# Input loads in order of need, rotated key channels on a second queue, and a last chunk that two engines normalise and one queue stores in four parts

## The chip, the cores and the metric

The kernel runs on one core of one Trainium2 chip. The metric is the device time of one execution in microseconds (us), lower is better. TensorE is called PE in the rows, VectorE DVE, ScalarE ACT, GpSimd POOL; SP is SyncE, which here only issues transfers. A row's L538 is line 538 of the kernel's source, and `out<-in` names the tensors.

## What is computed

One inference step of a two-layer decoder trunk in float32, for a prompt of 1024 tokens and 8 samples of 4 new tokens each, 1056 token columns in all. Cut to what matters:

```python
for l in range(2):                       # x <- LayerNorm(alpha * x + sublayer(x))
    z = x @ w_in                         # 1024 -> 22 (layer 0) or 37 (layer 1) tiles of 128 columns
    # layer 0: latent attention, linear recurrence, memory attention
    # layer 1: mLSTM, chunk MLP, memory attention
    x = layer_norm(alpha * x + mixed @ w_out, ln_g[l], ln_b[l])

# layer 0, the samples' latent attention over 16 pages of 128 cached tokens each:
def page_step(carry, pt):                # lat 256 channels, kr 32 rotated channels
    lat, kr = lat_pool[e, pt], rope_pool[e, pt]
    s = q_lat @ lat.T + q_rope @ kr.T
    return _softmax_accumulate(carry, s, lat), None
```

## The kernel before

Activations lie with channels on the 128 partitions (8 tiles `k`) and tokens along the columns, in three chunks `c` of 352 tokens. A float32 product is made of three matmuls: every operand is split into a rounded `hi` part (ACT) and the rest `lo` (DVE), and PE adds hi·hi, lo·hi and hi·lo (L538 to L540, L592 to L594). Each engine's program is written out by hand in its order; semaphores tie them together.

**Start.** PE's first products need `x_hi` and `x_lo` of chunk 0 and the first weight tile. SP loads chunk 0 of `x_raw` whole and then weights. POOL loads chunks 1 and 2, then six constants and the recurrence's weights `lru_w`. ACT and DVE split a chunk at a time. `pe_slot(t, c)` makes output tile `t` of chunk `c`; the order is (0, 0), (0, 1), (0, 2), (1, 0) and so on.

**Samples' latent attention** (`pe_mla_sample`). Ten events `EV`: in each group of four samples one for the new tokens and four for cached pages, each of those with 4 pages of 4 samples, numbered `r` = 0 to 7. For event `r` SP issues 16 page loads into one of three buffers (`pages[r % 3]`), once the values product of event `r - 3` is done (`ss_o`). A page row holds 256 latent and 32 rotated channels. PE first turns the pages over (`turn`, units `w` of 512 columns, moved out of PSUM by ACT and DVE in turn): 8 units of latent and a ninth, `w == 8`, of 16 small matmuls for the rotated channels (`ropeT`). Iteration `e` of the loop on PE is `turn(e+1)`, `transposes(e)`, `scores(e+1)`, `values(e)`.

**LayerNorm** of a chunk: PE sums the channels by a matmul with ones (`"sum"`, L731), DVE centres two halves of four tiles (L760), ACT squares them (L789), the squares are summed, ACT takes the root (L792), DVE the reciprocal (L769), DVE scales the halves (L772), ACT applies gain and bias tile by tile (L797). For chunks 0 and 1 DVE adds the 8 squared tiles first (L765, L766) and PE needs one matmul (L737); for the last chunk of each layer PE sums all 8 tiles itself (L742). In layer 0 the products (30, 0) stand between `"sum"` and `"square"` of that chunk, and (30, 1), (31, 0), (31, 1) behind them; (30, 2) waits for the whole normalised chunk 2. In layer 1 nothing is left beside this chain, and POOL stores each chunk of `y` whole, the last one as the program's last transfer.

Of the kernel before, what the change touches and what calls it, by code (L numbers as in the profile page):

```python
# [28 lines left out]
P = 128  # L29
# [112 lines left out]
def build(nc, x, o):  # L142

    with ExitStack() as ctx:
# [91 lines left out]
        page01 = keep("page", [P, 2, 4, 4, 288])  # L236
        latT = keep("latT", [P, 4, 2, 512])
        ropeT = keep("ropeT", [P, 512])
# [7 lines left out]
        page2 = place("page2", [P, 4, 4, 288], Z0 + 10 * ROWS)  # L246
# [112 lines left out]
        x_in = [sem(f"x_in{c}") for c in range(NCH)]  # L359
# [19 lines left out]
        lru_in = sem("lru_in")  # L379
# [30 lines left out]
        smp_in = sem("smp_in")  # L410
# [116 lines left out]
        def pe_slot(pe, t, c):  # L527
# [3 lines left out]
            if t in (0, 30, 31):  # L531
                pe.wait_ge(x_ready, NCH if t else c + 1)
                if t:
                    pe.wait_ge(x_ready, NCH + 2 * c + 2)
# [76 lines left out]
        def act_x_hi(act, c):  # L611

            act.activation(x_hi[:, :, chunk(c)], x_raw[:, :, chunk(c)], ACT.Copy).then_inc(x_hi_ready, 1)

        def dve_x_lo(dve, c):
            dve.wait_ge(x_hi_ready, c + 1)
            dve.tensor_tensor(x_lo[:, :, chunk(c)], x_raw[:, :, chunk(c)], x_hi[:, :, chunk(c)],
                              ALU.subtract).then_inc(x_ready, 1)
# [96 lines left out]

        def norm_at(table, n):

            return [(c, piece) for c in range(NCH - 1) for piece in table.get(n - KX * (c + 1), ())]
# [6 lines left out]
        def pe_norm(pe, l, c, what):  # L725
# [6 lines left out]
            else:  # L732
                if n:
                    pe.wait_ge(ln_r, n)
                if c < NCH - 1:
                    pe.wait_ge(ln_t, 2 * l + c + 1)
                    pe.matmul(bank(7, n=CH), ones[:, :], ln_sum[:, c % 2, :], start=True, stop=True).then_inc(ln_v, 1)  # L737
                    return
# [13 lines left out]
        def dve_norm_pieces(dve, v, l):  # L752
            def piece(c, what):
# [7 lines left out]
                elif what.startswith("sum"):  # L761
                    if c < NCH - 1:
# [3 lines left out]
                        dve.tensor_tensor(ln_sum[:, c % 2, :], ln_sq[:, 0, :], ln_sq[:, 1, :], ALU.add).then_inc(ln_t, 1)  # L766
                elif what == "root":
                    dve.wait_ge(ln_r, n + 1)
                    v.then(dve.reciprocal(root, root))  # L769
                elif what.startswith("scale"):  # L770
                    dve.wait_ge(ln_c, 2 * n + 2)
                    dve.tensor_tensor(r, r, wide(root), ALU.mult).then_inc(ln_n, 1)  # L772
                elif l == 0:
                    dve.wait_ge(x_hi_ready, NCH + 2 * c + h + 1)
# [4 lines left out]
        def act_norm_pieces(act, l):  # L779
            out = x_next if l == 0 else res  # L780

            def piece(c, what):
# [11 lines left out]
                elif what.startswith("affine"):  # L794
                    act.wait_ge(ln_n, 2 * n + h + 1)
                    for m in range(4 * h, 4 * h + 4):
# [401 lines left out]
        def pe_lru(pe, i, w):  # L1198
            j = LRU_ORDER[i]
            pe.wait_ge(lru_in, 16)  # L1200
# [71 lines left out]
        def dve_conv_edges(dve, v):  # L1272
            dve.wait_ge(z_free, ZI[(3, 2)])
            dve.wait_ge(branch_in, 32)
# [311 lines left out]
        def unit_out(n):  # L1586
            r, w = n // 9, n % 9
            if w == 8:
                return ropeT[:, :]
            return latT[:, w // 2, :, 256 * (w % 2):256 * (w % 2) + 256]  # L1590

        def unit_in(n):
            b = bank(UNIT_BANKS[n % 3])
            return b if n % 9 == 8 else b.rearrange("p (k c) -> p k c", k=2)

        def pe_mla_sample(pe):
# [3 lines left out]
            def turn(e):  # L1600
# [3 lines left out]
                for w in range(9):  # L1604
                    n = 9 * r + w
# [5 lines left out]
                    if w == 8:  # L1611
# [1351 lines left out]
```

## Time and profile before

| | us |
|---|---|
| median of three runs | 1580.4 (1580.4 to 1581.9) |
| the profiled execution, its own time | 1582.64 |
| its span, first to last event | 1580.9 |
| PE busy in the span | 1476.9 (93%) |
| DVE, ACT, POOL busy | 784.7, 577.5, 38.2 |

The span is what the rows count from. The other 1.74 us of the profiled execution lie outside it. Busy time of PE is modelled and pipelined, so 93% doesn't say that all of it is needed.

### The profile page before, as it was taken

How to read it: one execution, taken by the hardware profiler on the slowest of the kernel's cores; microseconds unless marked ns; L12 is line 12 of the kernel's file. 1: busy time of each engine (PE TensorE's matmuls, PEld its weight loads, DVE VectorE, ACT ScalarE, POOL GpSimd, SP SyncE). 2: the span in 40 equal slices, each digit the busy share in tenths (PEclk: the TensorE clock that was granted, in tenths of full speed). 3: DMA queues.
4: the chain of work that ended last, by engine and by line, in shares of the span. 5: the costliest groups of instructions: out<-in, count | busy, mean ns of one | idle time of the engine just before them, and what ended most of it. 6: DMA issues, size and time to landing. Idle time of an engine off the chain costs nothing.

```text
span 1580.9 us, 24315 instructions
## 1 busy us (share of the span) xinstructions
PE 1476.9 (93%) x10022; PEld 1298.7 (82%) x10022; DVE 784.7 (50%) x1444; ACT 577.5 (37%) x1030; POOL 38.2 (2%) x68
## 2 busy tenths in 40 slices
PE   5999999999999888889998999999999999999993
PEld 5988999866666565559997798999999989989992
DVE  3475643164554554555784143324444358526674
ACT  3057312144545554342453123204444115212343
POOL 1000000000000000000000100000000001000000
PEclk9999999999999999999998999999999899999997
DMA  5110032220001061735554230120011121114552
GB/s 198 42 40 28 28 108 94 74 82 13 1 1 54 1 185 49 203 124 167 168 191 165 94 107 28 49 52 27 28 30 57 70 81 41 42 39 149 170 190 73
DMA packets 51920, 132.13 MB, mean 84 GB/s; under 512 B 6601, under 2 KB 30394, under 8 KB 51042
## 3 DMA queue, kind: packets, MB, share of 16 engines
q1 hardware_dynamic: 46114, 111.45, 22.6%
q0 software_dynamic: 5696, 19.12, 3.3%
q8 instruction: 80, 1.31, 0.3%
q14 instruction: 30, 0.25, 0.1%
HBM read 117.08 MB, written 13.47 MB: 83 GB/s over the span
## 4 chain that ended last, share of the span: by engine, by line
PE 53%; DVE 3%; issue 2%; ACT 2%; POOL 0%; DVEq 0%; POOLq 0%; ACTq 0%
PE ps L538 9%; PE ps L540 9%; PE ps L539 9%; PE ps L592 4%; PE ps L593 4%; PE ps L594 4%; PE ps L1620 2%; PE ps L2051 1%; PE ps L1129 1%; PE ps L1645 1%; DVE ln_sq L769 1%; PE ps L2243 1%; PE ps L1917 1%; PE ps L1373 1%; PE ps L1915 1%
## 5 line engine op out<-in xcount | busy, mean ns | idle before, releaser
L538 PE MATMUL ps<-x_hi,w_hi 128*128 128x352 f32 x1416 | 472.8, 334 | 22.5 <-DVE w_lo L488 20.0
L540 PE MATMUL ps<-x_hi,w_lo 128*128 128x352 f32 x1416 | 458.6, 324 | 0.0
L539 PE MATMUL ps<-x_lo,w_hi 128*128 128x352 f32 x1416 | 458.1, 324 | 0.0
L538 PEld LDWEIGHTS ps<-x_hi,w_hi 128*128 128x128 f32 x1416 | 269.2, 190 | 32.0 <-DVE w_lo L488 20.3
L539 PEld LDWEIGHTS ps<-x_lo,w_hi 128*128 128x128 f32 x1416 | 270.0, 191 | 2.5 <-issue 1.2
L540 PEld LDWEIGHTS ps<-x_hi,w_lo 128*128 128x128 f32 x1416 | 268.8, 190 | 0.0
L482 ACT ACTIVATE w_hi<-w_raw 128x1024 fp32r<-128x1024 f32 (+1 forms) x107 | 123.3, 1152 | 311.0 <-PE ps L540 201.9
L488 DVE TENSOR_TENSOR w_lo<-w_raw,w_hi 128x1024 fp32r<-128x1024 f32 (+1 forms) x107 | 143.5, 1341 | 64.6 <-ACT w_hi L482 64.0
L592 PE MATMUL ps<-mx_hi,w_hi 128*128 128x352 f32 x480 | 158.1, 329 | 1.5 <-DVE mx_lo L679 1.2
L594 PE MATMUL ps<-mx_hi,w_lo 128*128 128x352 f32 x480 | 154.4, 322 | 0.0
L593 PE MATMUL ps<-mx_lo,w_hi 128*128 128x352 f32 x480 | 154.4, 322 | 0.0
L514 DVE COPY z<-ps 128x352 f32<-128x352 f32 x90 | 47.1, 524 | 194.2 <-PE ps L540 194.2
L502 ACT ACTIVATE sig<-ps 128x352 f32<-128x352 f32 x72 | 33.4, 464 | 200.4 <-PE ps L540 200.4
L592 PEld LDWEIGHTS ps<-mx_hi,w_hi 128*128 128x128 f32 x480 | 90.5, 189 | 3.0 <-DVE mx_lo L679 1.3
L593 PEld LDWEIGHTS ps<-mx_lo,w_hi 128*128 128x128 f32 x480 | 90.9, 189 | 0.8
L594 PEld LDWEIGHTS ps<-mx_hi,w_lo 128*128 128x128 f32 x480 | 90.4, 188 | 0.0
L516 DVE TENSOR_TENSOR mx<-sig,ps 128x352 f32<-128x352 f32 x54 | 28.1, 520 | 122.8 <-ACT sig L502 122.6
L918 ACT ACTIVATE probs<-ps,stat 128x1024 f32<-128x1024 f32 (+7 forms) x64 | 47.4, 741 | 98.2 <-DVE stat L948 97.7
L869 PE MATMUL ps<-kT,qT 96*128 96x512 f32 (+4 forms) x192 | 75.5, 503 | 0.5 <-ACT qs L2656 0.5
L881 PEld LDWEIGHTS ps<-ident,probs 128*128 128x128 f32 x288 | 32.8, 141 | 35.8 <-ACT probs L918 25.9
L881 PE MATMUL ps<-ident,probs 128*128 128x128 f32 x288 | 43.2, 277 | 16.5 <-ACT probsT L929 8.5
L601 DVE SCALAR_TENSOR_TENSOR res<-x_res,ps 128x352 f32<-128x352 f32 x48 | 24.9, 519 | 54.0 <-PE ps L594 54.0
(456 smaller groups left out, 1887.7 us busy)
## 6 DMA issues: line engine op xcount, KB each, us to landing
w_raw<-in_w_out SPq DMA_DIRECT2D x48, 640.0 KB, 3.9
w_raw<-in_w_in SPq DMA_DIRECT2D x59, 512.0 KB, 3.6
page<-in_cache_mla SPq DMA_DIRECT2D x128, 144.0 KB, 2.6
kvs<-in_mem_cache SPq DMA_DIRECT2D x16, 512.0 KB, 6.0
x_res<-in_xT SPq DMA_DIRECT2D x24, 176.0 KB, 2.4
x<-x_next POOLq DMA_DIRECT2D x3, 1408.0 KB, 8.1
x_res<-x SPq DMA_DIRECT2D x24, 176.0 KB, 2.3
out_y<-res POOLq DMA_DIRECT2D x3, 1408.0 KB, 5.9
```

The costliest lines, as they stand in the source:

```text
L482: act.activation(w_hi[:, u % 2, 0:n], w_raw[:, u % 2, 0:n], ACT.Copy).then_inc(w_hi_ready, 1)
L488: dve.tensor_tensor(w_lo[:, u % 2, 0:n], w_raw[:, u % 2, 0:n], w_hi[:, u % 2, 0:n], ALU.subtract).then_inc(w_split, 1)
L514: ins = dve.tensor_copy(out, zz[0:8] if tile.one else zz)
L538: pe.matmul(out, w_hi[:, u % 2, kk], x_hi[:, k, chunk(c)], start=(k == 0), stop=False)
L539: pe.matmul(out, w_hi[:, u % 2, kk], x_lo[:, k, chunk(c)], start=False, stop=False)
L540: mm = pe.matmul(out, w_lo[:, u % 2, kk], x_hi[:, k, chunk(c)], start=False, stop=(k == KX - 1))
L592: pe.matmul(out, w_hi[:, u % 2, kk], mx_hi[:, k, chunk(c)], start=(k == 0), stop=False)
L593: pe.matmul(out, w_hi[:, u % 2, kk], mx_lo[:, k, chunk(c)], start=False, stop=False)
L594: mm = pe.matmul(out, w_lo[:, u % 2, kk], mx_hi[:, k, chunk(c)], start=False, stop=(k == KM - 1))
L869: mm = pe.matmul(s[:, a:b], q_of(u), k_of(u, a, b), start=True, stop=True)
L881: mm = pe.transpose(ps[:, 4 + f % 2, (kt - k0) * P:(kt - k0 + 1) * P], pr[:, kt * P:(kt + 1) * P], ident[:, :])
L918: act.activation(probs_of(n, u), scores_of(n, u), ACT.Exp, bias=stat[:, n % 4:n % 4 + 1], scale=MLA_SCALE, accum_out=stat[:, 4 + n % 4:5 + ...
```

## The change

1. **Start.** The input comes in four parts (`X_PARTS`): tiles 0 to 3 of chunk 0, tiles 4 to 7 of chunk 0, chunk 1, chunk 2. All are issued by SP, with the first weight tile behind the first part and the second behind chunk 1. ACT and DVE split part by part; PE starts (0, 0) on part 0 and waits for part 1 before tile `k == 4`. POOL begins with the constants; `lru_w` and two small loads wait until the last input part has landed.
2. **Rotated channels.** The page rows are 256 wide. The rotated channels lie in an array of their own, laid out channels first, so they need no turning. POOL loads them, 128 transfers of 32 rows by 512 bytes, into three buffers, each group of four behind a read of page numbers into registers. The ninth unit is gone from PE, ACT and DVE.
3. **Squares.** For the last chunk DVE adds the squares, each half as soon as ACT has it (five instructions), and PE does one matmul.
4. **Last chunk of layer 1** (`LAST`). DVE scales tiles 0 to 3 as before and tile 4; tiles 5 to 7 it scales and biases itself. ACT does tiles 0 to 4. SP stores the last chunk of `y` in four parts, in the order in which they are ready.

```diff
+        X_PARTS = [(0, slice(0, 4)), (0, slice(4, KX)), (1, slice(0, KX)), (2, slice(0, KX))]
@@ pe_slot
+                if (t, c, k) == (0, 0, 4):
+                    pe.wait_ge(x_ready, 2)
@@ pe_norm, "square"
-                for m in range(KX):
-                    if m % 4 == 0:
-                        pe.wait_ge(ln_q, 2 * n + m // 4 + 1)
-                    mm = pe.matmul(bank(7, n=CH), ones[:, :], ln_sq[:, m, :], start=(m == 0), stop=(m == KX - 1))
-                mm.then_inc(ln_v, 1)
+                pe.wait_ge(ln_t, n + 1)
+                pe.matmul(bank(7, n=CH), ones[:, :], ln_sum[:, c % 2, :], start=True, stop=True).then_inc(ln_v, 1)
@@ dve_norm_pieces
+                    else:
+                        for g in range(2):
+                            dve.wait_ge(ln_q, 2 * n + g + 1)
+                            for a in (2, 1):
+                                v.then(dve.tensor_tensor(ln_sq[:, 4 * g:4 * g + a, :], ln_sq[:, 4 * g:4 * g + a, :],
+                                                         ln_sq[:, 4 * g + a:4 * g + 2 * a, :], ALU.add))
+                        dve.tensor_tensor(ln_sum[:, c % 2, :], ln_sq[:, 0, :], ln_sq[:, 4, :], ALU.add).then_inc(ln_t, 1)
+                elif what == "scale1" and (l, c) == LAST:
+                    dve.tensor_tensor(res[:, 4, chunk(c)], res[:, 4, chunk(c)], root, ALU.mult).then_inc(ln_n, 1)
+                    for m in range(A_TILES, KX):
+                        v.mark(dve.scalar_tensor_tensor(res[:, m, chunk(c)], res[:, m, chunk(c)],
+                                                        vec[:, V_LNG + KX * l + m:V_LNG + KX * l + m + 1], root,
+                                                        ALU.mult, ALU.mult))
+                    v.settle()
+                    for m in range(A_TILES, KX):
+                        dve.tensor_scalar(res[:, m, chunk(c)], res[:, m, chunk(c)],
+                                          vec[:, V_LNB + KX * l + m:V_LNB + KX * l + m + 1], None,
+                                          ALU.add).then_inc(ln_t, 1)
@@ pe_mla_sample, turn
-                    if w == 8:
-                        for q in range(4):
-                            for j in range(4):
-                                mm = pe.matmul(ps[32 * j:32 * j + 32, b, q * P:q * P + P],
-                                               pages[r % 3][:, q, j, LAT:LAT + ROPE], ident[:, :],
-                                               start=True, stop=True)
@@ pe_mla_sample, scores
+                pe.wait_ge(rp_in[real(e) % 3], 256 * (real(e) // 3 + 1))
@@ sync
+            for a, b, ready, n in ((0, 2, ln_y, KX * (2 * NCH - 1) + 2), (5, 7, ln_t, 2 * NCH + 2),
+                                   (2, 5, ln_y, KX * (2 * NCH - 1) + 5), (7, 8, ln_t, 2 * NCH + 3)):
+                sp.wait_ge(ready, n)
+                sp.dma_start(o["y"][:, a:b, chunk(NCH - 1)], res[:, a:b, chunk(NCH - 1)]).then_inc(out_done, 16)
+            sp.wait_ge(out_done, 64)
@@ gpsimd
-            for c in range(1, NCH):
-                gp.dma_start(x_raw[:, :, chunk(c)], x["xT"][:, :, chunk(c)]).then_inc(x_in[c], 16)
...
+            gp.wait_ge(x_in[3], 16)
+            gp.dma_start(lru_w, x["lru_w"].rearrange("p j w n -> p j (w n)")).then_inc(branch_in, 16)
...
+            gp.wait_ge(o_ready, len(PAIRS))
+            for r in range(8):
+                if r >= 3:
+                    gp.wait_ge(ss_o, 5 * ((r - 3) // 4) + 2 + (r - 3) % 4)
+                for j in range(4):
+                    n = (4 * (r // 4) + j) * NPG + 4 * (r % 4)
+                    _, four = nc.values_load_multi_w_load_instructions(
+                        table[0:1, n:n + 4], engines=[mybir.EngineType.Pool], min_val=0, max_val=NPHYS - 1,
+                        skip_runtime_bounds_check_because="a page table holds numbers of pages")
+                    for q in range(4):
+                        gp.dma_start(ropeT[32 * j:32 * j + 32, r % 3, q * P:q * P + P],
+                                     x["cache_rope"][bass.ds(four[q], 1), :, :].rearrange(
+                                         "a c p -> (a c) p")).then_inc(rp_in[r % 3], 16)
```

SP's program begins like this before the change (`w_raw` is a weight tile, two buffers):

```order
L2471 DMA x_raw<-in_xT 128x8x352
L474 DMA w_raw<-in_w_in 128x1024 [waits w_split] x16
L2477 DMA memT0a<-in_memT 128x1024 [waits lat_ready,conv_ready]
L2477 DMA memT0b<-in_memT 128x1024
L474 DMA w_raw<-in_w_in 128x1024 [waits w_split] x6
```

and like this after it:

```order
L2481 DMA x_raw<-in_xT 128x4x352
L474 DMA w_raw<-in_w_in 128x1024 [waits w_split]
L2481 DMA x_raw<-in_xT 128x4x352
L2484 DMA x_raw<-in_xT 128x8x352
L474 DMA w_raw<-in_w_in 128x1024 [waits w_split]
L2486 DMA x_raw<-in_xT 128x8x352
```

The whole input is now on SP's queue, in the order in which PE uses it. On PE, the iteration of the samples' attention with the second page event reads before the change:

```order
L1645 MATMUL ps<-latT,qs 32x512 x8
L1649 MATMUL ps<-ropeT,qsr 32x512 x4
L1675 MATMUL ps<-lat_tm,sp_selfT 32x256 x4
L1620 MATMUL ps<-ident,page 128x128 x32
L1614 MATMUL ps<-ident,page 32x128 x16
L1662 MATMUL ps<-ident,sp_p 128x128 x4
```

and after it, with L1654, L1658, L1684, L1628 and L1671 as the new numbers of L1645, L1649, L1675, L1620 and L1662:

```order
L1654 MATMUL ps<-latT,qs 32x512 x8
L1658 MATMUL ps<-ropeT,qsr 32x512 x4
L1684 MATMUL ps<-lat_tm,sp_selfT 32x256 x4
L1628 MATMUL ps<-ident,page 128x128 x32
L1671 MATMUL ps<-ident,sp_p 128x128 x4
```

Only the row of 16 small matmuls is gone. POOL's program after the change, from the stores of the prompt's memory keys and values to the first of the 128 loads of rotated channels:

```order
L1171 DMA out_mem_k<-km_90 128x2x256 [waits mem_ev]
L1172 DMA out_mem_v<-vm 128x2x256
L2593 DMA out_kr<-z 32x1056 [waits kr_ready]
L2601 TENSOR_LOAD table [waits o_ready,tbl_in]
L2605 ISA
L2605 DMA ropeT<-in_cache_rope 32x128
```

The last two rows stand four times behind each TENSOR_LOAD, and there are 32 such groups, four for each page event; the ISA row works out the address in registers. Before the change the store of `kr` was followed on POOL by the stores of `x_next`.

## Rows read from the trace of the kernel before

**Rows 1.** The page, part 4: shares of the chain that ended last, by engine.
```profile
PE 53%; DVE 3%; issue 2%; ACT 2%; POOL 0%; DVEq 0%; POOLq 0%; ACTq 0%
```

**Rows 2.** Timeline of the start: start us, us, engine, line, operation, [idle before <-releaser].
```profile
1.39 1.94 POOL L2553 DMA_DIRECT2D x_raw<-in_xT  x2 [0.86 <-POOLq L2937]
...
11.30 2.55 ACT L613 ACTIVATE x_hi<-x_raw 128x2816 fp32r<-128x2816 f32 x1 [9.21 <-DMA x_raw<-in_xT]
...
16.97 1.22 DVE L488 TENSOR_TENSOR w_lo<-w_raw,w_hi 128x1024 fp32r<-128x1024 f32 x1
18.10 6.19 DVE L617 TENSOR_TENSOR x_lo<-x_raw,x_hi 128x2816 fp32r<-128x2816 f32 x2
...
18.24 0.66 PE L538 MATMUL ps<-x_hi,w_hi 128*128 128x352 f32 x1 [18.24 <-DVE w_lo L488]
...
32.81 0.53 DVE L514 COPY z<-ps 128x352 f32<-128x352 f32 x1 [3.32 <-PE ps L540]
```

**Rows 3.** A window of 1 us: busy times, granted PE clock, DMA share, GB/s.
```profile
10.00:11.00 1.00, 0.00 (x0) 0.00 (x0) 0.00 (x0) 0.00 (x0) 0.00 (x0) 1.00 0.99 367
```

**Rows 4.** Timeline of one iteration of the samples' attention.
```profile
629.14 1.08 PE L1614 MATMUL ps<-ident,page 128*32 128x128 f32 x32
629.25 0.69 DVE L1779 COPY latT<-ps 128x512 f32<-128x512 f32 x1 [0.22 <-PE ps L1620]
...
630.15 0.66 PE L1662 MATMUL ps<-ident,sp_p 128*128 128x128 f32 x4
...
630.99 1.92 PE L1645 MATMUL ps<-latT,qs 128*32 128x512 f32 x16 [0.18 <-issue]
```

**Rows 5.** Page loads of `r = 3` and `r = 7`, last turn and scores; reads of numbers.
```profile
625.46 14.47 SPq L2515 DMA_DIRECT2D page<-in_cache_mla  x24
...
677.19 0.86 SPq L2515 DMA_DIRECT2D page<-in_cache_mla  x2
...
689.65 1.86 PEld L1620 LDWEIGHTS ps<-ident,page 128*128 128x128 f32 x16 [0.26 <-DMA page<-in_cache_mla]
...
693.67 1.92 PE L1645 MATMUL ps<-latT,qs 128*32 128x512 f32 x16 [0.32 <-DVE ropeT L1779]
...
L2504 SPq TENSOR_LOAD <-table x32: 293/296/504, 558.1 to 666.0; - x32
```

**Rows 6.** POOL's small transfers: timeline, then KB each and us to landing.
```profile
868.12 0.51 POOL L2584 DMA_DIRECT2D g_i<-gates  x1 [1.88 <-DMA gates<-mx]
...
g_i<-gates POOLq DMA_DIRECT2D x4, 4.0 KB, 1.8
g_f<-gates POOLq DMA_DIRECT2D x4, 4.0 KB, 5.1
```

**Rows 7.** Timeline of layer 0's normalisation: chunk 1's adds, then chunk 2.
```profile
809.11 2.54 DVE L765 TENSOR_TENSOR ln_sq<-ln_sq 128x1408 f32<-128x1408 f32 x2
...
834.10 3.15 DVE L760 SCALAR_TENSOR_TENSOR res<-ps,res 128x1408 f32<-128x1408 f32 x2
...
837.27 7.99 PE L742 MATMUL ps<-ln_sq,ones 128*128 128x352 f32 x16 [2.68 <-ACT ln_sq L789]
...
859.24 0.40 PE L538 MATMUL ps<-x_hi,w_hi 128*128 128x352 f32 x1 [2.53 <-DVE x_lo L775]
```

**Rows 8.** Timeline of the end, all engines.
```profile
1549.80 3.15 DVE L760 SCALAR_TENSOR_TENSOR res<-ps,res 128x1408 f32<-128x1408 f32 x2 [0.95 <-PE ps L731]
...
1552.98 6.66 PE L742 MATMUL ps<-ln_sq,ones 128*128 128x352 f32 x16 [3.22 <-ACT ln_sq L789]
...
1562.65 3.16 DVE L772 TENSOR_TENSOR res<-res,ln_sq 128x1408 f32<-128x1408 f32 x2
1564.31 4.68 ACT L797 ACTIVATE res<-res,vec 128x352 f32<-128x352 f32 x8 [4.08 <-DVE res L772]
1569.29 0.84 POOL L2550 DMA_DIRECT2D out_y<-res  x1 [17.91 <-ACT res L797]
```

**Rows 9.** DMA issues from 1545 us on: count, KB each, median us to landing.
```profile
out_y<-res POOLq DMA_DIRECT2D x2, 1408.0 KB, 5.9
```

More of the change, by code:

```diff
@@ L235, in build @@
         cursor[0] = X0
-        page01 = keep("page", [P, 2, 4, 4, 288])
+        page01 = keep("page", [P, 2, 4, 4, LAT])
+        ropeT = keep("ropeT", [P, 3, 512])
         latT = keep("latT", [P, 4, 2, 512])
-        ropeT = keep("ropeT", [P, 512])
         sp_p = keep("sp_p", [P, 2, 512])
@@ L409, in build @@
         pgT_ev = [sem("pgT_ev_a"), sem("pgT_ev_v")]
-        smp_in = sem("smp_in")
+        rp_in = [sem(f"rp_in{c}") for c in range(3)]
         l96_in = sem("l96_in")
@@ L609, in dve_step, with x_part, act_x_hi, dve_x_lo @@
                 dve.tensor_tensor(total, first, res[:, t, chunk(c)], ALU.add).then_inc(ln_a, 1)
[L611 to L618, printed above, removed]
+        def x_part(buf, n):
+            c, k = X_PARTS[n]
+            return buf[:, k, chunk(c)]
+        def act_x_hi(act, n):
+            act.wait_ge(x_in[n], 16)
+            act.activation(x_part(x_hi, n), x_part(x_raw, n), ACT.Copy).then_inc(x_hi_ready, 1)
+        def dve_x_lo(dve, n):
+            dve.wait_ge(x_hi_ready, n + 1)
+            dve.tensor_tensor(x_part(x_lo, n), x_part(x_raw, n), x_part(x_hi, n), ALU.subtract).then_inc(x_ready, 1)
         MX_ORDER = [4, 5, 6, 7, 8, 9, 0, 1, 2, 3]
@@ L795, in piece @@
                     act.wait_ge(ln_n, 2 * n + h + 1)
-                    for m in range(4 * h, 4 * h + 4):
+                    for m in range(4 * h, A_TILES if h and (l, c) == LAST else 4 * h + 4):
                         act.activation(out[:, m, chunk(c)], res[:, m, chunk(c)], ACT.Identity,
@@ L1603, in turn @@
                 r = real(e)
-                for w in range(9):
-                    n = 9 * r + w
+                for w in range(8):
+                    n = 8 * r + w
                     if w in (0, 4):
@@ L1648, in scores @@
                     rr = slice(32 * j, 32 * j + 32)
-                    mm = pe.matmul(ps[rr, e % 2, :], rows_of(qsr[rr], g, j), ropeT[rr, :], start=False, stop=True,
+                    mm = pe.matmul(ps[rr, e % 2, :], rows_of(qsr[rr], g, j), ropeT[rr, real(e) % 3, :], start=False, stop=True,
                                    skip_group_check=True)
@@ L1725, in units @@
                     return
-                first = 9 * real(e)
-                for n in range(first + first % 2, first + 9, 2):
+                first = 8 * real(e)
+                for n in range(first, first + 8, 2):
                     act.wait_ge(pgT_z, n + 1)
@@ L1775, in units @@
                     return
-                first = 9 * real(e)
-                for n in range(first + 1 - first % 2, first + 9, 2):
+                first = 8 * real(e)
+                for n in range(first + 1, first + 8, 2):
                     dve.wait_ge(pgT_z, n + 1)
@@ L2614, in _ @@
             gp.dma_start(o["chunk_v"], vd_s[:, :]).then_inc(cv_out, 16)
-            for c in range(NCH):
+            for c in range(NCH - 1):
                 gp.wait_ge(ln_y, KX * (NCH + c + 1))
@@ L2684, in _ @@
             v.then(dve.memset(eps[:, :], EPS))
-            for c in range(NCH):
-                dve_x_lo(dve, c)
-                if c == 0:
+            for n in range(len(X_PARTS)):
+                dve_x_lo(dve, n)
+                if n == 0:
                     dve_lo(dve, 0)
```

70 lines of the change are left out of this document (34 added, 36 removed).

## Prediction

> **What bounds the kernel now.** I read the chain of waits first: PE's own work is more than half of it and no other engine has more than 3% [rows 1], and the idle time left on PE lies in a few places. So time can be won only where PE waits or does work that another can take, and at both ends, where PE does nothing yet or any more. The timelines of four such places matter; reading down each of them, one looks for the row whose idle time names the releaser.
>
> *Start.* ACT can split chunk 0 only at 11.30, when the whole chunk has landed. Then x_hi, x_lo and w_lo follow one another, and PE begins at 18.24 [rows 2]. Meanwhile POOL's two 1.44 MB loads share the transfer engines with SP's. The transfers run at 367 GB/s together [rows 3]. Before 11.30 about 3.1 MB have to pass, chunk 0, as much of POOL's, and the constants' first part, so data begin near 3 us. The copy of the third slot starts at 32.81 [rows 2], so tile 1 begins about then; from there on PE has work.
>
> *Samples' attention.* PE does the turning, the transposes, the scores and the values one after another with next to no gap. The 16 small matmuls of the ninth unit run from 629.14 until the transposes begin at 630.15 [rows 4].
>
> *Layer 0's last chunk.* PE needs 7.99 us for the sum of squares, and three tiles and 15 us later it waits 2.53 us for `x_lo` of that chunk [rows 7].
>
> *End.* Centre to 1552.95, PE's squares, root, reciprocal, scale, affine, one POOL store at 1569.29 that lands 5.9 us later, at about 1575.2 [rows 8, 9]. The span ends 5.7 us after that, and I take this tail as fixed.
>
> **The change, part by part.**
>
> *Start.* Bytes in SP's order: part 0 0.72 MB, w0 0.52, part 1 0.72, chunk 1 1.44, w1 0.52, chunk 2 1.44; POOL's constants (0.27 MB) share the first of them. From 3.0 us at about 380 GB/s they land at about 6.0, 7.4, 9.2, 13.0, 14.4 and 18.2. A whole chunk costs ACT 2.55 and DVE 3.09, w_lo costs DVE 1.22 [rows 2]; half a chunk I take at half. So x_hi is ready at 7.4, x_lo at 9.0, w_hi at 8.5, w_lo at 10.2, and PE starts at about 10.3 instead of 18.24. That is not the gain, since it runs into later parts. Chunk 1: landed 13.0, x_hi 15.6, x_lo 18.7. Chunk 2: landed 18.2, x_hi 20.7, x_lo 23.8. Slot (0, 2) can begin at 23.9 and takes 24 x 0.16 = 3.9 us, ends at 27.8, where before it was about 32.8: **4.9 us**. w1 waits behind chunk 2 on ACT and DVE (x_lo ends 23.8, w_lo by 25.2), before 27.8. If a transfer is a microsecond late the gain is 3.9. Moving `lru_w` behind the input costs nothing: the recurrence needs it tens of microseconds later.
>
> *Ninth unit.* 630.15 - 629.14 = 1.01 us of PE goes in each of 8 turns. The scores behind it then wait for the last latent unit: DVE's copy ends at 629.94 [rows 4], the transposes, started 1.01 earlier, end at 629.8. So the scores begin at 629.99 instead of 630.99, and nearly all of it is kept: 8 x 1.01 = 8.1 us. What is late next is the page load. A load may start when the values of `r - 3` are done; for the last event SP issues its 16 loads from 677.19 on, two in 0.86 us, and PE already waits 0.26 us for the second half at 689.65 [rows 5]. Between the two PE now saves one more unit (1.01), while the loads, bound by SP's issue and not by their bytes, are hardly quicker. That wait grows by 1.0. The event `r = 3` has some 1 us to spare by the same count. Net: **7.1 us** (8.1 if the smaller pages are quicker).
>
> *Rotated channels on POOL.* This operation is not in the trace. A small POOL transfer takes 0.51 us, landing 1.8 to 5.1 us [rows 6]. A read of four page numbers takes SP 0.29 to 0.50 us [rows 5]. Per event there are 16 issues and 4 reads; C is what they take together. Lower bound, if all register work hides behind the issues: 16 x 0.51 = 8.2 us. Upper bound from these rows: SP's page loads take 0.33 each and start 0.53 apart (the second of two ends 0.86 after the first begins [rows 5]), so 0.2 lies between them; 16 x 0.71 + 4 x 0.5 = 13.4. I take the middle for the issue and the short read, 16 x 0.61 + 4 x 0.3 = 11, since both are the same kind of work on the same kind of sequencer, and landing L = 3. POOL may begin an event when SP may. For r = 7 that was 677.19 and the scores came at 693.67 [rows 5], 16.5 us later; two units go from between, 14.4 are left, the same for r = 3. Needed: 11 - 0.5 + 3 = 13.5, just in time. The backlog: from r = 3's start at 625.46 to the last scores there were 68.2 us, six units fewer make 62.1, and POOL's last transfer lands 5C - 0.5 + L after that start if events queue up. PE is then late by 5C + L - 62.6: nothing for C = 11, from C = 11.9 on 5 us for each microsecond. I take **0 us**; 7 at C = 13.4, and 9 with a landing of 5.1. What waits behind it on POOL, the stores of `x_next`, comes 90 us later.
>
> The Trainium skill, "DMA: Bandwidth & Descriptors", section "Latency and other measured facts", gives a register read from memory a floor of about 600 ns. By it C would be 12.2 and PE 1.4 us late, an estimate from that page; the rows say 0.29 to 0.50, so the sum doesn't take it.
>
> *Squares.* Two adds of 1408 and 704 columns take 2.54 us [rows 7], one of 1408 takes 1.6 [rows 8], so 704 costs 0.92; 352 columns cost 0.53 [rows 2]. 2 x (0.92 + 0.53) + 0.53 = 3.45 after the centre, then one matmul of about 0.9. Layer 0: the centre ends at 837.25, so the sum is there at 841.6 instead of 845.26: 3.6 us earlier. PE's own three tiles then start at 841.3 and take 11.6 us, perhaps 1.5 more if the granted clock is the lower one after the idle time, so they end by 854.4, before `x_lo` at 855.6: **3.6 us**. Bounds 2 to 5, the upper if PE's shorter wait before (30, 2) spares it a stretch at the lower clock. Layer 1: 1552.95 + 3.45 + 0.9 = 1557.35 instead of 1559.64: **2.3 us**.
>
> *Scaling and store.* From the reciprocal on, before: two halves, 3.16, and 8 affines beside them, the last done at 1568.99 [rows 8], 6.3 us after the scaling began. Now ACT has 5 (1.6 + 5 x 0.585 = 4.6) and DVE 1.6 + 0.53 + 3 x 0.53 + 3 x (0.26 to 0.53) = 4.5 to 5.3. Gain 1.3. The store: POOL's whole one took 5.9 us from an issue 0.3 behind. Now a first part is on its way 2 us before, and 1.08 MB of the 1.44 follow within a microsecond: at 370 GB/s 2.9 us and a start of 1.2, about 4.2 from the last issue. Gain 1.7. **3.0 us** (1 to 4).
>
> Sum: 4.9 + 7.1 + 0 + 3.6 + 2.3 + 3.0 = 20.9. From the profiled execution's 1582.6 that is 1561.7; the median of the runs shown lies 2.2 below that execution, so 1580.4 - 20.9 = **1559.5**.
>
> **Rivals.**
>
> *Forecast:* POOL keeps up. For it: small issues of 0.5 us, and the first three events have 40 us. 0.57.
>
> *POOL falls behind a little.* C = 12.5 to 15.5: 5C + 3 - 62.6 = 3 to 18 us come back, time 1562 to 1577, at C = 14 1570. The upper end is beyond the bound above, since no row shows register work on POOL. For it: POOL's address work has no row, and three page events and one with new tokens run behind one another. 0.23. The Trainium skill, "SBUF — State Buffer", section "SBUF: two separate sides", says that descriptors of POOL's transfers are not written while DVE runs a copy from SBUF to SBUF in its two-port mode. DVE's copies in this stage read PSUM, so by it nothing changes here; it could fall on the first groups only.
>
> *Slower.* Each issue with its register work takes 0.95 us, as POOL's big ones do (two in 1.94 [rows 2]): C = 15.2 + 4 x 0.4 = 16.8, late by 24, minus 20.9 gives 1584. It decides from C = 16.2 on. Against it: those moved 1024 rows each, these 32. 0.05.
>
> *Less at the ends.* The transfers at the start are issued by one queue and cannot keep 380 GB/s, the parts land 2 us later, and four stores take as long as one: 4 to 5 us less, 1564. 0.08.
>
> *More.* No low clock behind the shorter waits, smaller pages load quicker: 1556. 0.07.
>
> **The numbers.** Two runs differ by up to 0.1%; 0.2% (3.2 us, 1577.2 to 1583.6) is what tells a change from none. Faster: 0.57 + 0.07 + 0.08 + nearly all of 0.23, and 0.93 in all; within 0.2%: 0.02; slower: 0.05. The range takes in the forecast (1557 to 1562), the better case and POOL's lateness up to C = 14: 1555 to 1570.
>
> **What would show it.** PE's first matmul near 10.3 and the third slot's copy near 27.8; no ninth unit and no wait of PE on `ropeT`; a wait on `page` of about 1.3 us at the last turn; POOL's issues 0.5 to 0.65 us apart, with C readable from one event; layer 0's single L737-like matmul ending near 841.6 less what went before; in the end 4.2 us from SP's last issue to landing. The prediction is wrong if POOL's pitch passes 0.7 us, if loads on two queues slow the pages, or if the 5.7 us behind the last landing depend on which queue stored.

## The result and the profile after

| | before | after |
|---|---|---|
| median, us | 1580.94 (4 runs, 1580.4 to 1581.9) | 1563.91 (4 runs, 1561.34 to 1566.23) |
| ratio | | 0.9893, 95% interval 0.9879 to 0.9907 |
| profiled execution, span | 1580.9 | 1564.6 |
| PE busy | 1476.9 | 1462.9 |
| POOL busy | 38.2 | 99.2 |

The change is worth 17.0 us in the median and 16.3 in the two spans. The forecast was 1559.5, 4.4 below the result, with 20.9 us as its sum. That looks close, but the terms are not: in these two traces the samples' attention gave 1.5 us for a term of 7.1, and the end gave twice its terms, through something that the prediction had called fixed.

The timeline of the start of the changed kernel, as in [rows 2], and the copy of the third slot behind it:

```profile
5.63 1.38 ACT L619 ACTIVATE x_hi<-x_raw 128x1408 fp32r<-128x1408 f32 x1 [3.42 <-DMA x_raw<-in_xT]
...
8.66 1.22 DVE L488 TENSOR_TENSOR w_lo<-w_raw,w_hi 128x1024 fp32r<-128x1024 f32 x1
...
9.93 0.66 PE L540 MATMUL ps<-x_hi,w_hi 128*128 128x352 f32 x1 [9.93 <-DVE w_lo L488]
...
18.93 2.56 ACT L619 ACTIVATE x_hi<-x_raw 128x2816 fp32r<-128x2816 f32 x1 [2.63 <-DMA x_raw<-in_xT]
...
29.05 0.52 DVE L514 COPY z<-ps 128x352 f32<-128x352 f32 x1 [2.17 <-PE ps L542]
```

PE starts at 9.93 instead of 18.24, and the third slot's copy stands at 29.05 instead of 32.81. That is a lead of 3.8 us, and only this lead counts.

The last turns of the samples' attention, PE's timeline, against the last two of [rows 5]:

```profile
664.40 1.92 PE L1654 MATMUL ps<-latT,qs 128*32 128x512 f32 x16 [0.55 <-DVE latT L1788]
...
674.13 1.92 PE L1654 MATMUL ps<-latT,qs 128*32 128x512 f32 x16 [0.55 <-DVE latT L1788]
...
681.76 2.00 PE L1628 MATMUL ps<-ident,page 128*128 128x128 f32 x16 [0.91 <-DMA page<-in_cache_mla]
...
687.14 3.35 PE L1654 MATMUL ps<-latT,qs 128*32 128x512 f32 x16 [2.94 <-DMA ropeT<-in_cache_rope]
```

And GpSimd's issues, which feed that last row:

```profile
661.93 1.07 POOL L2605 DMA_DIRECT2D ropeT<-in_cache_rope  x2 [0.43 <-issue]
663.34 1.08 POOL L2605 DMA_DIRECT2D ropeT<-in_cache_rope  x2 [0.34 <-issue]
670.20 2.22 POOL L2605 DMA_DIRECT2D ropeT<-in_cache_rope  x4 [5.77 <-PE ps L1686]
...
680.67 0.50 POOL L2605 DMA_DIRECT2D ropeT<-in_cache_rope  x1 [0.19 <-issue]
```

Three things are to be seen. A turn now takes 9.7 us (664.40 to 674.13) where it took 10.5. The scores of `r = 7` stand 2.94 us for their rotated channels, and the 16 matmuls behind that wait take 3.35 us in place of 1.92: the granted clock is 0.55 from 687.0 to 690.4, close to the lower of TensorE's two levels. And GpSimd was not slow. It stood idle for 5.77 us before it could begin `r = 7`, released by L1686, the weighted sum of `r = 4` (reading the first page numbers is part of this time). The 16 issues of the event take it 11.0 us (670.20 to 681.17), and PE goes on 6.5 us after the last of them began.

The end, all engines, against [rows 8]:

```profile
1544.16 3.16 DVE L760 SCALAR_TENSOR_TENSOR res<-ps,res 128x1408 f32<-128x1408 f32 x2 [0.95 <-PE ps L738]
...
1547.23 1.44 DVE L771 TENSOR_TENSOR ln_sq<-ln_sq 128x704 f32<-128x704 f32 x2
...
1550.32 0.52 DVE L773 TENSOR_TENSOR ln_sum<-ln_sq 128x352 f32<-128x352 f32 x1
1550.99 1.51 PE L743 MATMUL ps<-ln_sum,ones 128*128 128x352 f32 x2 [6.86 <-DVE ln_sum L773]
1552.54 0.55 ACT L810 ACTIVATE ln_sq<-ps,eps 128x352 f32<-128x352 f32 x1 [3.81 <-PE ps L743]
...
1557.17 2.97 ACT L815 ACTIVATE res<-res,vec 128x352 f32<-128x352 f32 x5 [4.08 <-DVE res L790]
...
1558.45 2.86 SPq L2561 DMA_DIRECT2D out_y<-res  x4
1559.09 1.03 DVE L785 TENSOR_SCALAR res<-res,vec 128x352 f32<-128x352 f32 x3
```

And what the transfer engines moved in the last 7 us, 1558 to 1565, in 40 slices of 0.175 us:

```profile
GB/s 0 0 0 0 0 0 0 56 346 378 362 370 370 177 0 80 362 330 330 394 354 370 370 378 362 378 386 386 378 362 346 330 266 16 0 0 0 0 0 0
```

The last byte passes at about 1563.8 (in the 34th slice), and the span ends at 1564.6. In the kernel before, the same view of 1571 to 1581 has its last byte at 1574.8, and the span ends at 1580.9. So of the 10.7 us that the end gained (27.95 us from the centring's end to the span's end before, 17.3 after), 5.3 are what lay behind the last byte, 6.1 before and 0.8 after.

### The profile page after: what moved, and what is told of

Its sections match the earlier page's. It is cut to its first block, busy times and chain, and to the rows that moved or that the text cites. A ratio compares the mean times of both kernels' runs of the same rounds, so it can differ in the third digit from the quotient of the medians.

```text
span 1564.6 us, 24181 instructions
## 1 busy us (share of the span) xinstructions
PE 1462.9 (93%) x9738; PEld 1290.3 (82%) x9738; DVE 789.8 (50%) x1457; ACT 573.9 (37%) x1024; POOL 99.2 (6%) x193
## 4 chain that ended last, share of the span: by engine, by line
PE 82%; DVE 8%; ACT 4%; issue 4%; DMA 1%; SPq 1%; POOLq 0%; POOL 0%; ACTq 0%; DVEq 0%
PE ps L540 14%; PE ps L542 14%; PE ps L541 14%; PE ps L594 4%; PE ps L596 4%; PE ps L595 4%; PE ps L887 2%; PE ps L911 2%; PE ps L1147 2%; PE ps L899 2%; DVE stat L965 1%; PE ps L1628 1%; PE ps L2821 1%; PE ps L2060 1%; PE ps L2830 1%
## 5 line engine op out<-in xcount | busy, mean ns | idle before, releaser
L2605 POOL DMA_DIRECT2D ropeT<-in_cache_rope x128 | 63.6, 497 | 285.8 <-issue 239.1
```

The source lines that it names most:

```text
L2605: gp.dma_start(ropeT[32 * j:32 * j + 32, r % 3, q * P:q * P + P], x["cache_rope"][bass.ds(four[q], 1), :, :].rearrange("a c p -> (a c) p") ...
```

## Experiments

Every kernel ran beside the kernel before on the same chip. On one chip single times of the kernel before lie up to 9.6 us apart (1576.38 to 1585.99), so small differences are read from the traces as well, at the same place in the program; a trace is one execution, and where it and the median disagree, the text says so.

### Whose tail is it?

Four kernels ask what the 6 us behind the last byte belong to.

`y_on_sp`, the kernel before with one store moved:

```
             sp_steps(sp, 1)
+            sp.wait_ge(ln_y, 2 * KX * NCH)
+            sp.dma_start(o["y"][:, :, chunk(NCH - 1)], res[:, :, chunk(NCH - 1)]).then_inc(out_done, 16)
+            sp.wait_ge(out_done, 16)
...
-            for c in range(NCH):
+            for c in range(NCH - 1):
                 gp.wait_ge(ln_y, KX * (NCH + c + 1))
                 store(o["y"][:, :, chunk(c)], res[:, :, chunk(c)])
```

> The kernel before, with one edit: the last chunk of y is still scaled as before and stored whole, but by SyncE. Theory A (5.7 us tail of a GpSimd store, 0.3 of one of SyncE): 5 to 6 us faster than before, 1575 us. Rival C (the tail belongs to any end of the program): within 1 us of before, 1580 us.

`pool_waits`, the changed kernel with one wait more:

```
             gp.wait_ge(gout_done, n_out[0])
+            gp.wait_ge(out_done, 64)
```

> The changed kernel, whose GpSimd waits at its very end for the four stores of y that SyncE issued, as SyncE does. Between the last byte of y and the end of the span lay some 5.7 us in the kernel before (last store issued by GpSimd) and some 0.3 us in the changed one. Theory A (the 5.7 us belong to a store that GpSimd's queue carries): no change against the changed kernel, end of the span within 0.6 us of the last landing. Rival B (GpSimd is slow to finish once its last wait is met, whoever issued the store): 4 to 6 us slower than the changed kernel, 1568 to 1570 us.

`four_on_pool`, the changed kernel, the four stores and their waits moved from SyncE's program to the end of GpSimd's stores, where they count on `gout_done`:

```
...
-                sp.wait_ge(ready, n)
-                sp.dma_start(o["y"][:, a:b, chunk(NCH - 1)], res[:, a:b, chunk(NCH - 1)]).then_inc(out_done, 16)
-            sp.wait_ge(out_done, 64)
...
+                gp.wait_ge(ready, n)
+                n_out[0] += 16; gp.dma_start(o["y"][:, a:b, chunk(NCH - 1)], res[:, a:b, chunk(NCH - 1)]).then_inc(gout_done, 16)
```

> The changed kernel, whose four parts of the last y are issued by GpSimd, with the same waits in the same order. GpSimd's issue of a large store lasts 0.85 us, SyncE's some 0.4 to 0.9. Theory A (a store of GpSimd's queue has some 5 us behind its last byte): 5 to 8 us slower than the changed kernel, 1569 to 1572 us, with 5 to 6 us between the last landing and the span's end. Rival C (the end is shorter because it is cut in parts and two engines scale, as the prediction had it, with the queue worth nothing): within 2 us of the changed kernel.

`sp_waits`, the kernel before, the last store still GpSimd's, but counted on `out_done`, for which SyncE waits and GpSimd doesn't:

```
+            sp.wait_ge(out_done, 16)
...
-            for c in range(NCH):
+            for c in range(NCH - 1):
...
+            gp.wait_ge(ln_y, 2 * KX * NCH)
+            gp.dma_start(o["y"][:, :, chunk(NCH - 1)], res[:, :, chunk(NCH - 1)]).then_inc(out_done, 16)
```

> The kernel before: GpSimd stores the last y whole as before, but SyncE waits for its landing in place of GpSimd, whose own last wait is for the earlier stores. So far: GpSimd stores and waits, 6.2 us from the last byte to the span's end; SyncE stores and waits, 0.8 us; SyncE stores, both wait, 7.2 us. Theory A (GpSimd needs 6 to 7 us to finish after its last instruction, and overlaps them with the store here): GpSimd is through with its issue at 1570.1 and finishes at 1576 to 1577, SyncE at 1576: 4 to 5 us faster than before, 1575 to 1577 us. Rival B (what is late is a GpSimd queue that has just carried a store): no change, 1580 us.

| kernel | stores | waits for it | last byte | span's end | between | median, ratio to before |
|---|---|---|---|---|---|---|
| before | GpSimd | GpSimd | 1574.8 | 1580.9 | 6.1 | |
| y_on_sp | SyncE | SyncE | 1573.3 | 1574.1 | 0.8 | 1574.47, 0.9959 (0.9945 to 0.9972) |
| after | SyncE | SyncE | 1563.8 | 1564.6 | 0.8 | 1563.91, 0.9893 |
| pool_waits | SyncE | both | 1562.3 | 1569.5 | 7.2 | 1570.70, 0.9935 (0.9918 to 0.9952) |
| four_on_pool | GpSimd | GpSimd | 1561.8 | 1569.3 | 7.5 | 1572.24, 0.9948 (0.9928 to 0.9967) |
| sp_waits | GpSimd | SyncE | 1574.4 | 1577.8 | 3.4 | 1579.04, 0.9995 (0.9982 to 1.0008) |

`pool_waits` decides between the two theories of the first three, and against the one that I had put first. Nothing about the stores differs from the changed kernel there; only GpSimd waits for them too. The end of that kernel, 1560 to 1570, in slices of 0.25 us:

```profile
GB/s 383 372 372 366 372 366 377 355 344 113 0 0 0 0 0 0 0 0 0 0 0 0 0 0 0 0 0 0 0 0 0 0 0 0 0 0 0 0 0 0
```

The transfers are over in the tenth slice, and the span goes on for 7.2 us in which no engine has a row. So the time belongs to GpSimd's own finish after its last wait, and not to a store on its queue. What GpSimd does in it no row shows. `sp_waits` is the converse and half a confirmation. GpSimd's last row is its issue, which ends at 1569.89, and the span ends 7.9 us later; had the tail begun at the last byte (1574.4), the end would be at 1580.5. From the start of that issue to the end of the span it took 8.7 us there and 11.6 before, 2.9 less, where 4 to 5 were expected. The median moved by 0.6 us alone, within an interval that reaches from 2.8 us faster to 1.3 slower, so the 2.9 us rest on the two traces. A GpSimd that issues the last store still ends late. Moving the store and the wait together is what paid: 5.3 us behind the last byte in `y_on_sp`, and about 6 in its median, as theory A had it.

### Each part by itself

The kernel before with one part of the change's diff at a time, word for word. Only in the last one two counts differ, since `ln_t` has two increments fewer without the third part:

```
-            for a, b, ready, n in ((0, 2, ln_y, KX * (2 * NCH - 1) + 2), (5, 7, ln_t, 2 * NCH + 2),
-                                   (2, 5, ln_y, KX * (2 * NCH - 1) + 5), (7, 8, ln_t, 2 * NCH + 3)):
+            for a, b, ready, n in ((0, 2, ln_y, KX * (2 * NCH - 1) + 2), (5, 7, ln_t, 2 * NCH),
+                                   (2, 5, ln_y, KX * (2 * NCH - 1) + 5), (7, 8, ln_t, 2 * NCH + 1)):
```

> The kernel before with the first part of the change alone: input in four parts in order of need, constants and lru_w from GpSimd. The prediction had 4.9 us for it (3.9 if a transfer is late); the changed kernel's trace shows its third slot's copy at 29.05 in place of 32.81, 3.8 us, and the same lead still there at 600. Theory A (that lead is kept to the end): 3.5 to 4 us in the trace at every mark, 1576 to 1577 us. Rival B (the lead is lost where a transfer is the limit): less than 2 us at the end of the span.

> The kernel before with the second part alone: pages without rotated channels, these loaded by GpSimd. From the first turning matmul to the first matmul of the out-projection the stage took 106.1 us before, 104.6 in the changed kernel and 99.8 where the buffer is freed by the scores. Theory A (the late release of the buffer eats the gain): 103 to 106 us for the stage, a wait of 2 to 4 us on ropeT at the last turn, and 1 to 3 us faster in all. Rival B (only together with the other parts is it late, since they move when loads meet): 99 to 101 us for the stage, 5 to 7 us faster in all.

> The kernel before with the third part alone: VectorE adds the last chunks' squares, TensorE sums one tile. The prediction had 3.6 us in layer 0 and 2.3 in layer 1, 5.9 in all. In the changed kernel layer 0 gained 2.9 us up to the root, 4.4 up to the gates' store and again 2.9 from 900 on. Theory A: 2.9 us kept from layer 0 and 2.3 to 3 from layer 1, 1574 to 1576 us. Rival B (what PE saves it waits for later): under 1.5 us from layer 0, 1577 to 1579 us.

> The kernel before with the fourth part alone: the last third scaled by two engines and stored in four parts by SyncE. From the end of the centring to the span's end it took 27.9 us before and 17.3 in the changed kernel, of which adding the squares on VectorE is some 2.7. Theory A (GpSimd needs some 6 us to finish after its last wait, SyncE under 1): 19.5 to 20.5 us, 8 us faster, 1572 to 1573 us. The prediction's sum (tail fixed, 1.3 + 1.7 us): 3 us faster, 1577 us.

| kernel | median | ratio to before | us |
|---|---|---|---|
| start_only | 1578.72 | 0.9993 (0.9981 to 1.0004) | -1.7 |
| rope_only | 1580.31 | 0.9992 (0.9977 to 1.0008) | -0.1 |
| squares_only | 1577.71 | 0.9987 (0.9976 to 0.9998) | -2.7 |
| end_only | 1571.63 | 0.9940 (0.9918 to 0.9962) | -8.8 |

The fourth part has more than half of the gain, and the rotated channels on GpSimd give nothing that the medians can show (from 3.6 us faster to 1.3 slower), where 1 to 3 us were expected. The four add up to 13.3 us, the whole gives 17.0; each has 1.7 to 3.5 us of uncertainty, so this is no contradiction, nor a proof that they are independent.

In `start_only` the lead is 4.4 us at the first store of the conv state (65.12 against 69.53), 5.8 at 201, 3.9 at 904 and 2.2 at the end. It grows and shrinks in stretches of code that are the same in both. The windows between two of GpSimd's stores, before and `start_only` (us; PE, PEld, DVE, ACT, POOL busy; PEclk, DMA share, GB/s):

```profile
1220.42:1294.91 74.49, 74.49 (x417) 67.31 (x416) 36.21 (x58) 8.60 (x13) 1.31 (x3) 0.91 0.18 61
```

```profile
1216.52:1292.69 76.17, 76.17 (x417) 68.97 (x416) 36.22 (x58) 8.60 (x13) 1.31 (x2) 0.89 0.17 60
```

The same 417 matmuls, PE without a pause in both, take 1.7 us longer at a mean granted clock of 0.89 than at 0.91. So in the trace rival B (a transfer is the limit) is not what took the lead. Over the 14 profiles of this study, all with this same code, the stretch took 74.5 to 74.6 us in seven and 76.0 to 76.2 us in seven.

The median says less than theory A expected: 1.7 us, and its interval ends at 3.0. The runs' clocks say where some of the lead may have gone. The ten runs of `start_only` have mean granted clocks of 0.975 to 0.979, 0.9767 on average, the 25 of before on the same chip 0.977 to 0.984, on average 0.9799; and among those 25 a clock lower by 0.001 goes with a time 1.0 us longer. By these numbers the lower clock costs `start_only` some 3 us (an estimate). `squares_only` has 0.9767 too, `rope_only` 0.9792. Why a kernel whose start is earlier meets the lower clock more often is not shown.

`rope_only` confirms that the wait comes with the second part alone: 2.5 us on `ropeT` at the last turn, 1.3 on `page`, the stage 102.0 us.

`squares_only` has layer 0's 2.85 us as the changed kernel (between GpSimd's second and third store of `x_next` 22.06 us against 24.90, and 22.05 after). In layer 1 the time from the second to the third store of `y` went from 18.76 to 17.19: 1.6 us. That is 4.4 us in the trace, where the median has 2.7 (interval 0.3 to 3.8), a value that rival B had named. The other traces show why the first number is not a fixed one. With the squares added on VectorE the stretch in layer 0 takes 22.05 to 22.10 us in every trace. With the 16 matmuls it takes 24.9 us in four traces and 23.6 and 23.4 in `end_only` and `rope_only`, where the 16 matmuls ran in 6.7 and 6.5 us in place of 8.0 (mean granted clock 0.75 in `end_only`, 0.62 in before). So this part is worth 2.85 us or 1.4 in layer 0, as the clock falls. `end_only` took 19.6 us from centring to the span's end, inside the 19.5 to 20.5 of theory A, and 3 us faster is excluded.

### The wait on the rotated channels

`rope_free` is the changed kernel with one word changed. The last reader of a `ropeT` buffer is the scores (`ss_z`); the weighted sum (`ss_o`) comes 10 us later and reads the page only:

```
                 if r >= 3:
-                    gp.wait_ge(ss_o, 5 * ((r - 3) // 4) + 2 + (r - 3) % 4)
+                    gp.wait_ge(ss_z, 5 * ((r - 3) // 4) + 2 + (r - 3) % 4)
```

> The changed kernel; GpSimd's rotated channels of page group r wait for the scores of group r-3 (the last reader of the ropeT buffer) and no longer for its weighted sum. In the changed kernel's trace the group r=7 was issued only from 670.20, after 5.77 us of waiting for the weighted sum of r=4, took 11.0 us, and landed 5.9 us behind its last issue; the scores of r=7 stood 2.94 us and then ran 16 matmuls in 3.35 us in place of 1.93. Theory A (the buffer's release is what made it late): GpSimd runs through without a pause from some 664 us, the wait is gone, the 1.4 us of low clock and perhaps 1.7 us of slow matmuls behind it too: 3 to 6 us faster than the changed kernel, 1558 to 1561 us, and its runs no longer fall in two groups 4 us apart. Rival B (the small transfers land late because they share the DMA engines with the pages, whose r=7 group lands just as late: 0.91 us of waiting for them in the changed kernel): a wait for the pages takes the place of most of it, less than 1.5 us faster, 1562 to 1565 us.

The median was 1561.47 (1557.22 to 1563.09), ratio 0.9874 (0.9854 to 0.9895). GpSimd began `r = 7` at 660.09 in place of 670.20, and PE has no wait on `ropeT` left, 0.32 us on `page`:

```profile
660.09 2.22 POOL L2605 DMA_DIRECT2D ropeT<-in_cache_rope  x4 [5.68 <-PE ps L1658]
```

It was repeated beside the changed kernel itself:

> The changed kernel once more, on the same chip and beside the next one. Ten profiles so far show the same code at full or half clock in places that differ from one execution to the next, 1.5 us apart each time. Theory A (its runs spread by 4 us for that reason): median 1562 to 1565 us, spread 5 us or more over ten runs, and in its trace the wait on ropeT of 1.5 to 3 us or a longer wait for the pages. Rival B: the two groups were something of that chip, and the spread is under 2 us.

> The changed kernel with ropeT released by the scores, once more, beside the changed kernel itself. Theory A (the wait on ropeT goes and nothing takes its place): 2.5 to 4 us faster than the changed kernel in the median, 1559 to 1561 us. Rival B (the first pair of medians, 1563.9 and 1561.5, was chance): within 1 us.

1562.73 (1558.69 to 1564.93) for the changed kernel and 1560.79 (1558.69 to 1562.44) with the release: 1.9 us, less than the 2.5 to 4 expected, and within what two such medians differ by chance. The changed kernel's four runs spread over 6.2 us, as theory A there had it. The times alone don't prove the release's worth; the stage in the traces does. One window each, from the first matmul after the prompt's attention to the first of the out-projection, in the columns of the windows above: before, then `y_on_sp` (its code up to there is that of before):

```profile
601.00:707.08 106.08, 92.94 (x1130) 58.36 (x1128) 57.18 (x112) 47.10 (x90) 0.00 (x0) 0.95 0.43 125
```

```profile
601.72:705.15 103.43, 90.15 (x1131) 55.60 (x1129) 57.14 (x112) 47.06 (x90) 0.00 (x0) 0.98 0.44 129
```

The changed kernel twice:

```profile
597.60:702.22 104.62, 85.12 (x874) 52.22 (x873) 54.55 (x108) 44.74 (x86) 39.72 (x80) 0.93 0.43 127
```

```profile
598.93:701.13 102.20, 82.57 (x874) 49.56 (x872) 54.54 (x108) 44.66 (x86) 39.71 (x80) 0.96 0.44 130
```

`rope_free`, `rope_free_again`:

```profile
598.67:698.43 99.76, 83.38 (x874) 51.92 (x872) 54.56 (x108) 44.74 (x86) 39.71 (x80) 0.95 0.46 133
```

```profile
597.59:697.57 99.98, 83.39 (x874) 51.91 (x872) 54.54 (x108) 44.75 (x86) 39.71 (x80) 0.94 0.46 133
```

The column before the last two is the clock, the first number behind the length is PE's busy time. One and the same code takes 106.1 us at 0.95 and 103.4 at 0.98, the changed one 104.6 at 0.93 and 102.2 at 0.96. Three more kernels have the changed code in this stage: `rope_only` takes 102.0 us at 0.96, `pool_waits` 102.1 at 0.95, `four_on_pool` 99.9 at 0.98. Length alone can't tell the release from the clock, since 99.9 is what `rope_free` has at 0.95.

PE's idle time (length less busy time) can. It is 18.4 to 19.6 us in the five traces of the changed code and 16.4 and 16.6 with the release. In the five, PE stands 2.9 to 4.0 us for `page` and `ropeT` together over the stage, not always for the same one: `pool_waits` stands 2.9 us for `page` and not at all for `ropeT`. With the release it is 0.3 and 0.5, all of it for `page`. So the late release costs this stage 2 to 3 us. The rest of what the profiled execution lost is its clock: PE was busy for 85.1 us there and for 82.6 in the second trace of the same kernel.

`rope_first` goes on from there. In every turn of these kernels PE stands 0.55 us for VectorE's copy of the last latent unit, while the rotated channels' matmuls, which don't need it, stand behind. It has the release too, and the order:

```
+                pe.wait_ge(rp_in[real(e) % 3], 256 * (real(e) // 3 + 1))
+                for j in range(4):
+                    rr = slice(32 * j, 32 * j + 32)
+                    pe.matmul(ps[rr, e % 2, :], rows_of(qsr[rr], g, j), ropeT[rr, real(e) % 3, :], start=True, stop=False,
+                              skip_group_check=True)
                 for par in range(2):
                     pe.wait_ge(pgT_ev[par], 4 * (real(e) + 1))
-                pe.wait_ge(rp_in[real(e) % 3], 256 * (real(e) // 3 + 1))
                 for k in range(2):
                     for j in range(4):
...
-                                  start=(k == 0), stop=False, skip_group_check=True)
+                                       start=False, stop=(k == 1), skip_group_check=True)
```

> The changed kernel with ropeT released by the scores, and in each turn's scores the rotated channels' matmuls (8 in 1.06 us) put ahead of the latent ones. In the changed kernel PE stands some 0.55 us in every turn for VectorE's copy of the last latent unit; these matmuls don't need it. Theory A (the turn is then bound by PE's own work): turns of 9.2 us in place of 9.75, 8 x 0.55 = 4.4 us, less about 1 us as the pages of the last turn come later against it: the stage 2.5 to 4.4 us shorter than the 99.8 to 100.0 with the buffer's release alone, 1557 to 1559 us. Rival B (the page loads bound the last turns, and what a turn saves is waited for there): the wait on page grows from 0.3 to 0.5 us to 3 us or more, the stage less than 1.5 us shorter, 1560 to 1561 us.

Median 1555.25 (1552.10 to 1555.57), ratio 0.9830 (0.9816 to 0.9843): the fastest of all, 25.8 us below before. PE's timeline of one turn and of the wait that is left, and the stage:

```profile
657.92 1.06 PE L1652 MATMUL ps<-ropeT,qsr 32*32 32x512 f32 x8
658.91 1.92 PE L1658 MATMUL ps<-latT,qs 128*32 128x512 f32 x16
...
666.90 1.06 PE L1652 MATMUL ps<-ropeT,qsr 32*32 32x512 f32 x8
667.89 1.92 PE L1658 MATMUL ps<-latT,qs 128*32 128x512 f32 x16
...
674.70 2.00 PE L1628 MATMUL ps<-ident,page 128*128 128x128 f32 x16 [1.23 <-DMA page<-in_cache_mla]
```

```profile
596.08:690.94 94.86, 81.62 (x875) 51.02 (x873) 54.59 (x108) 44.74 (x86) 39.71 (x80) 0.95 0.49 140
```

A turn takes 9.0 us (657.92 to 666.90) and its idle time is gone; the stage is 4.9 us shorter than with the release alone, at the same clock, a little more than the 2.5 to 4.4 expected. Of the 4.9, 3.1 are idle time and 1.8 are busy time of PE, which no run explains. Rival B appears in small: PE waits 0.90 us for the pages of `r = 3` and 1.23 for those of `r = 7`, 2.1 in all. That is the next wait that a change would meet in this stage.

## Why the prediction came out as it did

**Start: 4.9 forecast, 3.8 measured.** The mechanism and PE's start (9.93 against 10.3) were right. The third chunk's split began at 18.93, 0.7 later than the landing that I had reckoned with; and I set the end of the slot (27.8) against the old copy's time (32.81), where the copy stands 0.5 behind the slot. The bound of 3.9 named for a late transfer was the value.

**Ninth unit: 7.1 forecast, 6.1 to 6.3 measured.** That is how much shorter the stage is with the wait removed, at about the clock of before, so the term was nearly right. I had the scores follow the last copy by 0.05 us. In the trace they start 0.25 behind it, which makes PE's idle time there 0.55 instead of 0.18 to 0.32 [rows 4, 5] in most turns, and so a turn gains 0.8 or less and not 1.0. The page wait of 1.3 that I had named at the last turn was 0.91.

**Rotated channels on GpSimd: 0 forecast, 2 to 3 us measured.** This is the step that failed. C, what GpSimd needs for one event, was nearly right: 11 taken, 10.7 for each of `r = 3` to `r = 6` (621.53 to 664.42) and 11.0 for `r = 7` (16 issues of 0.50 each, 0.07 to 0.33 between them, 0.43 to 0.60 at most reads of four numbers). For `r = 7` 0.8 us come on top: SyncE began to load its pages at 669.38, GpSimd its rotated channels at 670.20, behind its first read. L was wrong: 3 taken, 6.5 from the start of the last issue to the matmul. The rows that I had named held landings up to 5.1 [rows 6]; with 5.1 the event alone comes to 15.6 us against the 14.4 there were, so the term was 0 only by the choice of the short one.

The long landing goes with other loads. SyncE's are under way too (its page loads ran from 669.38 for 8.44 us, two of `w_raw` came behind them). In the five traces in which this event starts late, the longest landing of a transfer of rotated channels is 5.8 to 6.3 us; in the three in which it starts early it is 3.8 to 3.9. The pages suffer as well: their second half reaches PE 12.4 to 13.5 us after SyncE began to issue them in the five, and 11.8 to 12.0 in the three. Which of SyncE's loads holds up the last small ones no run separates.

The sum asked how fast the queue is and not what it waits for: it had 5.77 us of waiting in front of that very event, for a release that the buffer didn't need. The rival "POOL falls behind a little" had this lateness and at its lower end this price, but another cause, a C of 12.5 or more, which no row shows. The Trainium skill, "DMA: Bandwidth & Descriptors", section "Latency and other measured facts", gives a read from memory into a register a floor of about 600 ns. GpSimd's 32 reads of page numbers took 0.31 to 0.53 us here, 0.32 in the median, so this trace does not show that floor, and the sum was right not to take it.

**Squares: 3.6 + 2.3 forecast, 2.85 + 1.5 measured.** The adds took 3.5 us as reckoned (3.45). The sum over the partitions took 1.51 us in place of 0.9, in both layers: it comes behind 6.3 and 6.9 us in which PE has nothing, and runs at a granted clock of 0.50, the lower of TensorE's two levels, 1.2 GHz. Before, the first of the matmuls that it replaces came after 2.7 and 3.2 us [rows 7, 8]. The 2.85 are measured against a trace in which those took 8.0 us; against the two in which they took 6.5 and 6.7, layer 0 gains 1.4.

**Scaling and store: 3.0 forecast, 3.8 measured.** From the root to the last scaled tile 9.3 us became 7.6 (1.7 for 1.3), from there to the last byte 5.8 became 3.7 (2.1 for 1.7).

**The tail: fixed at 5.7 forecast, 5.3 us gained.** "I take this tail as fixed" was wrong, and its error is what saved the total. It was a stretch without rows whose cause I had not asked for, and the text named it only as a way to be wrong. That the total came out near is luck. The end gave 10.7 us for the 5.3 of its terms (2.3 and 3.0).

**Where the rest went.** At 702 the profiled execution was 4.9 us ahead, at the centring of chunk 2 (831.06 against 834.10) 3.0. In between lies the out-projection, the same code: its first 4 us ran at a granted clock of 0.50 against 0.60, the next 4 at 0.86 against 1.00, and behind them SyncE's loads of `x_res`, one per slot, came every 4.83 us instead of 4.77, 0.9 us over the stage at a clock of 1.00 in both. Of this last I have no cause.

The whole, from one mark to the next in the two profiled executions: start 3.8, up to 600 us -0.4, stage 1.5, out-projection -1.8, squares of layer 0 2.9, from there to 1545 -0.3, end 10.7; 16.4, and the spans differ by 16.3. Right were the mechanism of the start, the cost of GpSimd's issues and the splitting at the end. Wrong was the landing of the rotated channels behind a late release: with it the stage gained about 4 us in place of 7 (102.1 in `pool_waits` against 106.1, both at 0.95), and at the 0.93 of the profiled execution 1.5. One unseen gain of 5.3 made up for it.

## What to carry to other kernels

Before a transfer's throughput is reckoned, look for what releases its buffer: the right semaphore is that of the last reader, and one word was worth 2 to 3 us here. Put what needs no fresh operand ahead of what waits for the last copy; that made this stage 4.9 us shorter. And let GpSimd's last wait be met early: in this program whatever it waits for last had 6 to 8 us behind it in which nothing was computed, while SyncE added under 1.

## What the hardware showed unexpectedly

GpSimd's finish: 6.1, 7.2 and 7.5 us from the last byte to the span's end when it waits for it, 7.9 from its last issue where only SyncE waits for that store, 0.8 from the last byte where SyncE stores and waits alone. No row shows what GpSimd does in this time.

TensorE's clock: the same code runs through the samples' attention at a mean granted clock of 0.95 or 0.98 and takes 106.1 or 103.4 us. The changed kernel's own two profiles have 0.93 and 0.96 there. The 16 matmuls of the squares in layer 0 take 8.0 us in four traces and 6.5 and 6.7 in two. One profile a kernel is then too little for a term of 2 us: compare the same stretch of code in several, with the clock beside it, and PE's idle time apart from its busy time.
